# A two-block model kernel on one core: each slab product as three products of 256 columns into one sum, and two pairs of PSUM banks in turn

## The chip, the cores and the metric

One core of a Trainium2 chip. The metric is the device time of one execution in microseconds (us). The kernel before took 2976.21 us, the median of three runs (2973.67 to 2978.57).

## The reference

256 tokens of width 2048 go through four blocks of layers, all weights in fp32:

```
h = h + hybrid_layer(rmsnorm(h), ...)      # h @ w_in, gated delta rule + dilated attention, @ w_out
h = h + shortconv_layer(rmsnorm(h), ...)   # h @ w_in, short convolution, @ w_out
...                                        # second part: an input product, state-space branch,
                                           # block attention with 8 heads, gates, merge, @ w_out
h = h + ff(norm(h))                        # w_ff1 (2048 x 8192), relu(x)*x, w_ff2 (8192 x 2048)
out = rmsnorm(h)
```

Nearly all the arithmetic is weights times 256 tokens. To keep fp32 accuracy with the fast number format of the multiplying engine (fp32r), each operand is split into a high part and a low part, and a product is high*high + high*low + low*high.

## The kernel before

**Slabs and groups.** The weights stream from memory as slabs of 128x1024 fp32 (512 KB): 2 chunks of the inner dimension (k) by 4 chunks of 128 output columns (n). A ring of 4 slots holds raw slabs. ScalarE copies a slab to its high part (`wh`, L1007), VectorE subtracts to get the low part (`wl`, L1568; GpSimd does some, L1496). `walk` (L370) is the schedule of a group on ScalarE and VectorE: at each slab it splits the slab three ahead, calls hooks for the other work of the layer (two hook slots for a slab), and runs the tail of the group at places given by `tail_at`. The order of all work is written out by hand; there is no planner.

**The product.** `group` (L545) runs on TensorE. For each slab and each n it makes four products, here called a block: two with `wh` as weights (k = 0, 1) over 512 columns, which hold the high and the low part of the activations side by side, and two with `wl` over the 256 high columns. There are 3744 such blocks in the program (936 slabs by 4).

```
mm(G[n][:, :],      wh[...], rhs(k))             # 512 columns: high | low
mm(G[n][:, T:2*T],  wl[...], rhs(k)[:, 0:T])     # 256 columns, added to the second half
```

Each output chunk n has one PSUM bank `G[n]` of 512 columns: the first half is high*high, the second half the two mixed products. A group of 4, 8 or 12 slabs sums in these four banks; there are 122 groups. When it ends, `evac` on ScalarE (L1017) copies the second half of each bank to `tmp`, and `add` on VectorE (L1573) adds the first half and writes the result. Where the result goes into the residual stream, `into_x` does both steps on VectorE (L1592 or L1594, then L1600 or L1602). The add of bank n increments `bank_freed`; the next group's first product into bank n waits for it.

**Who else waits.** In the hybrid layer a head's delta rule runs beside the products of the next head, three groups (gi = 0, 1, 2) for a head, with hooks at numbered slots (`DELTA_AT`). Step 7 of the delta rule stands at slot 14, just before the second half of gi = 0's tail on VectorE: a chain of small operations (L1756, L1758, L1796). Its result goes out to memory and comes back (`act.dma_start` at L1128 to L1133, semaphore `base_moved`), and TensorE's step 10 at slot 22 (L682) waits for it. Loops are real loops on the engines (`Fori`): on TensorE one of 7 passes with three groups (heads), one of 6 passes with four groups (short convolution, L823), and several in the feed-forward part.

Of the kernel before, what the change touches and what calls it, by code (L numbers as in the profile page):

```python
# [106 lines left out]
def program(nc, stack, ins, out_d):  # L107
# [22 lines left out]
    tmp = place("tmp", [P, 4, T])  # L130
# [212 lines left out]
    tmp_ready = sem("tmp_ready")  # L343
# [43 lines left out]
    HEADS_ACT, HEADS_DVE = (1, 2), (0, 2)  # L387
    EVAC_ACT, EVAC_DVE = (1, 1), (0, 1)
# [71 lines left out]
    def group_of(pair, e):  # L460

        return 8 * (pair // 4) + 2 * (pair % 2) + pair % 4 // 2 + 4 * e

# [73 lines left out]
    def _(pe):  # L537
        mm = nc.tensor.matmul

        def group(g, q0, nslabs, rhs, ready, hook=None, slot0=0):  # L540

            for sl in range(nslabs):
# [251 lines left out]
        for gi in range(3):  # L794
            group(gi, 2 * gi, 8, xs_of, xs_wait(0), lambda slot: gates(GATE_PE.get(slot)), 16 * gi)
        pe.wait_ge(loads["hyb"], 32)

        with pe.Fori(1, QK_HEADS) as h:
            for gi in range(3):
                group(3 * h + gi, 6 * h + 2 * gi, 8, xs_of, lambda sl: None, heads(h - 1), 16 * gi)  # L800
# [8 lines left out]
        for gi in range(3):  # L809
            group(G_OUTA + gi, Q_OUTA + 2 * gi, 8, hid_of(outa_chunks), outa_ready, heads(7), 16 * gi)  # L810
        group(G_OUTA + 3, Q_OUTA + 6, 8, hid_of(outa_chunks), outa_ready)
# [5 lines left out]
        for i in range(4):  # L817
            group(G_OUTB + i, Q_OUTB + i, 4, hid_of(outb_chunks), outb_ready,
# [4 lines left out]
        with pe.Fori(0, N_SC_ITER) as j:  # L823
            for gi in range(4):
                group(G_SC + 4 * j + gi, Q_SC + 8 * j + 2 * gi, 8, xs_of, xs_wait(1))
# [5 lines left out]
        for i in range(4):  # L831
            group(G_SCOUT + i, Q_SCOUT + 3 * i, 12, lambda k: hid[:, k, :], sc_ready,
# [30 lines left out]
        for i in range(2):  # L863
            group(G_U + i, Q_U + 2 * i, 8, xs_of, xs_wait(2), before_ssm, 16 * i)
# [1679 lines left out]
```

## Time and profile before

| | before |
|---|---|
| median of 3 runs | 2976.21 us |
| the profiled execution, its own time | 2972.52 us |
| its span in the profile | 2970.7 us |
| TensorE busy | 2877.3 us (97%), 16934 products and as many weight loads |
| VectorE, ScalarE, GpSimd busy | 2170.2 us (73%), 1480.7 us (50%), 453.7 us (15%) |
| chain that ended last | TensorE 63%, "issue" 26%, VectorE 7%, ScalarE 3%, DMA 1% |
| DMA | 636.93 MB, mean 214 GB/s |

PE is TensorE's products, PEld its weight loads, which run beside the products; DVE is VectorE, ACT is ScalarE, POOL is GpSimd, SP the engine that issues most transfers. The end of a product is modelled and includes its way through the array, so neighbouring products overlap in the records: what a product costs in a stream is the distance from its start to the next one's start, not its duration. Where rows are merged (x2), the duration runs from the first start to the last end.

### The profile page before, as it was taken

The numbers are of one execution on the slowest core, as the hardware profiler recorded it, in microseconds if no ns is written. First come the engines' busy times: TensorE is split into PE (matmuls) and PEld (weight loads), VectorE is DVE, ScalarE is ACT, GpSimd is POOL, SyncE is SP. The second block draws the span as 40 slices with busy tenths as digits, with TensorE's granted clock in tenths as the row PEclk, the third lists the DMA queues.
The fourth block names the chain that finished last, engine by engine and source line by source line (L and its number), as shares of the span: only waits on it lengthen the run. The fifth ranks groups of instructions, "written<-read, shape, count | busy, mean of one in ns | idle before, by whom it ended". The sixth has DMA issues, their size and how long they took to land.

```text
span 2970.7 us, 50332 instructions
## 1 busy us (share of the span) xinstructions
PE 2877.3 (97%) x16934; PEld 2502.1 (84%) x16934; DVE 2170.2 (73%) x3182; ACT 1480.7 (50%) x2124; POOL 453.7 (15%) x188
## 2 busy tenths in 40 slices
PE   7999999999999999999999999999999999999998
PEld 6888888888888888888887877788888888888887
DVE  6677767777679888888877989976787436465466
ACT  4444444444344444444444777766544444444443
POOL 0111011111000000000000000000003445545443
PEclk9999999999999999999999999999999999999999
DMA  6544444445457888788875445556684666766655
GB/s 219 168 140 151 157 147 154 159 148 178 156 198 287 305 311 305 284 317 305 307 275 181 165 164 174 166 198 217 243 319 157 198 211 226 249 232 238 207 184 177
DMA packets 199089, 636.93 MB, mean 214 GB/s; under 512 B 32312, under 2 KB 46776, under 8 KB 198208
## 3 DMA queue, kind: packets, MB, share of 16 engines
q1 hardware_dynamic: 165024, 601.92, 58.4%
q10 hardware_dynamic: 33952, 33.52, 3.5%
q8 instruction: 69, 1.13, 0.2%
q14 instruction: 44, 0.36, 0.0%
HBM read 619.61 MB, written 15.75 MB: 214 GB/s over the span
## 4 chain that ended last, share of the span: by engine, by line
PE 63%; issue 26%; DVE 7%; ACT 3%; DMA 1%; DVEq 0%; ACTq 0%; SPq 0%; POOL 0%; POOLq 0%
PE gemm L552 39%; PE gemm L557 20%; DVE wl L1568 2%; ACT wh L1007 1%; DVE dT L1758 1%; DVE dW L1756 1%; DMA raw<-in_stream 0%; DVE qkv L1742 0%; PE side L708 0%; DVE cb L1573 0%; DVE xs L1657 0%; PE side L578 0%; DMA x<-in_x 0%; PE side L698 0%; PE side L682 0%
## 5 line engine op out<-in xcount | busy, mean ns | idle before, releaser
L552 PE MATMUL gemm<-xs,wh 128*128 128x512 f32 x5120 | 1627.6, 399 | 45.6 <-DVE cb L1573 21.2
L1007 ACT ACTIVATE wh<-raw 128x1024 fp32r<-128x1024 f32 x939 | 983.4, 1058 | 997.7 <-PE gemm L557 863.1
L1568 DVE TENSOR_TENSOR wl<-raw,wh 128x1024 fp32r<-128x1024 f32 x811 | 1034.4, 1280 | 460.1 <-ACT wh L1007 439.1
L557 PEld LDWEIGHTS gemm<-xs,wl 128*128 128x128 f32 x5120 | 965.4, 189 | 214.6
L557 PE MATMUL gemm<-xs,wl 128*128 128x256 f32 x5120 | 1015.0, 280 | 0.0
L552 PEld LDWEIGHTS gemm<-xs,wh 128*128 128x128 f32 x5120 | 781.5, 189 | 77.4 <-issue 44.0
L552 PE MATMUL gemm<-hid,wh 128*128 128x512 f32 x2368 | 745.8, 396 | 11.1 <-DVE xacc L1600 4.6
L557 PEld LDWEIGHTS gemm<-hid,wl 128*128 128x128 f32 x2368 | 446.1, 188 | 100.8
L557 PE MATMUL gemm<-hid,wl 128*128 128x256 f32 x2368 | 467.9, 279 | 0.0
L1496 POOL TENSOR_TENSOR wl<-raw,wh 128x1024 fp32r<-128x1024 f32 x128 | 349.4, 2735 | 365.3 <-ACT wh L1007 365.3
L552 PEld LDWEIGHTS gemm<-hid,wh 128*128 128x128 f32 x2368 | 357.0, 188 | 14.6 <-DVE xacc L1600 4.1
L1502 POOL TENSOR_TENSOR rn<-nrm,mhalf 128x2 f32<-128x2 f32 (+1 forms) x5 | 3.8, 760 | 1458.4 <-DVE nrm L1634 773.1
L1017 ACT ACTIVATE tmp<-gemm 128x256 f32<-128x256 f32 x408 | 152.2, 379 | 67.5 <-PE gemm L557 58.9
L1915 DVE SCALAR_TENSOR_TENSOR ada_a<-ada_a,cond 128x1024 f32<-128x1024 f32 x144 | 175.5, 1219 | 0.0
L1573 DVE TENSOR_TENSOR fx<-gemm,tmp 128x256 f32<-128x256 f32 x96 | 38.4, 421 | 80.2 <-ACT tmp L1017 78.2
L1522 POOL TENSOR_TENSOR rn<-nrm,mhalf 128x4 f32<-128x4 f32 x8 | 14.8, 1851 | 498.2 <-DVE nrm L1825 498.2
L1915 DVE SCALAR_TENSOR_TENSOR ada_b<-ada_b,cond 128x1024 f32<-128x1024 f32 x48 | 76.2, 1587 | 0.0
L2179 DVE TENSOR_TENSOR t<-side,CS 128x1024 f32<-128x1024 f32 x32 | 39.0, 1219 | 2.2 <-PE side L895 1.7
L2187 DVE TENSOR_TENSOR_SCAN rr<-mag,t 128x256 f32<-128x256 f32 x64 | 40.5, 675 | 0.0
L2192 DVE TENSOR_TENSOR crs<-rr,CS 128x1024 f32<-128x1024 f32 x32 | 39.2, 1225 | 1.1
L1742 DVE SCALAR_TENSOR_TENSOR qkv<-cb,vec,qkv 128x256 f32<-128x256 f32 x96 | 40.0, 479 | 0.0
L895 PE MATMUL side<-uT,lbt 32*128 32x256 f32 x256 | 37.2, 409 | 0.6 <-DVE lbt L2120 0.6
(393 smaller groups left out, 1801.9 us busy)
## 6 DMA issues: line engine op xcount, KB each, us to landing
raw<-in_stream SPq DMA_DIRECT2D x940, 512.0 KB, 4.1
ada_a<-in_ada SPq DMA_DIRECT2D x144, 512.0 KB, 5.2
ada_b<-in_ada SPq DMA_DIRECT2D x48, 512.0 KB, 5.3
stash<-stage ACTq DMA_DIRECT2D x12, 512.0 KB, 3.4
att<-stash ACTq DMA_DIRECT2D x8, 384.0 KB, 3.9
x<-in_x SPq DMA_DIRECT2D x4, 512.0 KB, 5.8
A_scratch<-gB ACTq DMA_DIRECT2D x8, 256.0 KB, 3.5
Dm<-D_scratch ACTq DMA_DIRECT2D x8, 256.0 KB, 3.8
```

What stands on the lines that cost most here:

```text
L552: mm(G[n][:, :], wh[:, slot, at:at + P], rhs(sl * SLAB_K + k), start=sl == 0 and k == 0, stop=False, skip_group_check=True)
L557: op = mm(G[n][:, T:2 * T], wl[:, slot, at:at + P], rhs(sl * SLAB_K + k)[:, 0:T], start=False, stop=last, skip_group_check=True)
L1007: A(wh[:, slot, :], raw[:, slot, :], ACT.Copy).then_inc(hi_ready, 1)
L1017: A(tmp[:, n, :], G[n][:, T:2 * T], ACT.Copy).then_inc(tmp_ready, 1)
L1496: nc.gpsimd.tensor_tensor(wl[:, slot, :], raw[:, slot, :], wh[:, slot, :].bitcast(F32), ALU.subtract).then_inc(lo_ready[slot], 1)
L1568: tt(wl[:, slot, :], raw[:, slot, :], wh[:, slot, :].bitcast(F32), ALU.subtract).then_inc(lo_ready[slot], 1)
L1573: tt(out, G[n][:, 0:T], tmp[:, n, :], ALU.add).then_inc(bank_freed, 1)
L1742: op = stt(qkv[:, n, :], src, w, qkv[:, n, :], ALU.mult, ALU.add)
L1915: stt(s_, s_, 0.5, cond[:, half * SLAB:half * SLAB + SLAB], ALU.mult, ALU.mult, accum_out=parts[:, bass.ds(t0 + m, 1)]).then_inc(S("ada_us ...
L2179: tt(t1[:, :, :, :], bu, CS[:, b, :, :, :], ALU.mult).then_inc(S("m_t1"), 1)
L2187: op = nc.vector.tensor_tensor_scan(rr[:, e, :], mag[:, g:g + 1].to_broadcast([P, T]), t1[:, e, 0, :], 0.0, ALU.mult, ALU.add)
L2192: tt(crs[:, b, :, :, :], rr[:, :, :].unsqueeze(2).to_broadcast([P, 2, 2, T]), CS[:, b, :, :, :], ALU.mult).then_inc(S("m_crs"), 1)
```

## The change

- A block now is six products of 256 columns, all added in the same 256 columns of PSUM: for each k `wh` times high and `wh` times low, then for each k `wl` times high. Two chunks n share a bank (columns 0 to 255 and 256 to 511).
- The four banks form two pairs. A group uses one pair; the next group uses the other. A group waits until the pair was freed by the group two before it; only the first group of a head (gi = 0) follows one on the same pair and waits for that one (`back=1`).
- `evac` on ScalarE and the buffer `tmp` are gone. On VectorE one copy of 128x512 (`take`) empties a bank, that is two chunks, and `into_x` needs one operation for each chunk.
- `bank_ready` is raised once for a group (after n = 1) in place of three times. Loops of the feed-forward part run over pairs of groups.

```diff
-        def group(g, q0, nslabs, rhs, ready, hook=None, slot0=0):
+        def group(g, pair, q0, nslabs, rhs, ready, hook=None, slot0=0, back=2):
...
                 for n in range(SLAB_N):
-                    if sl == 0:
-                        wait(pe, bank_freed, 4 * g + n - 3)
+                    if sl == 0 and n % 2 == 0:
+                        wait(pe, bank_freed, 4 * (g - back) + n + 2)
+                    o = bank(pair, n)
                     for k in range(SLAB_K):
-                        at = (k * SLAB_N + n) * P
-                        mm(G[n][:, :], wh[:, slot, at:at + P], rhs(sl * SLAB_K + k), start=sl == 0 and k == 0,
-                           stop=False, skip_group_check=True)
+                        w = wh[:, slot, (k * SLAB_N + n) * P:(k * SLAB_N + n + 1) * P]
+                        moving = rhs(sl * SLAB_K + k)
+                        mm(o, w, moving[:, 0:T], start=sl == 0 and k == 0 and n % 2 == 0, stop=False, skip_group_check=True)
+                        mm(o, w, moving[:, T:2 * T], start=False, stop=False, skip_group_check=True)
                     for k in range(SLAB_K):
-                        at = (k * SLAB_N + n) * P
+                        w = wl[:, slot, (k * SLAB_N + n) * P:(k * SLAB_N + n + 1) * P]
                         last = sl == nslabs - 1 and k == SLAB_K - 1
-                        op = mm(G[n][:, T:2 * T], wl[:, slot, at:at + P], rhs(sl * SLAB_K + k)[:, 0:T], start=False,
-                                stop=last, skip_group_check=True)
+                        op = mm(o, w, rhs(sl * SLAB_K + k)[:, 0:T], start=False, stop=last, skip_group_check=True)
                     if n == SLAB_N - 1:
                         op.then_inc(slab_used, 1)
-                    elif sl == nslabs - 1:
+                    elif sl == nslabs - 1 and n == SLAB_N // 2 - 1:
                         op.then_inc(bank_ready, 1)
...
+    def bank(pair, n):
+
+        return G[2 * pair + n // 2][:, n % 2 * T:n % 2 * T + T]
+
+    def pair_of(position):
+
+        return (position + 1) % 2
...
-        def evac(g, q_end, half=None):
-
-            for n in range(SLAB_N) if half is None else (2 * half, 2 * half + 1):
-                if n < SLAB_N - 1:
-                    act.wait_ge(bank_ready, 3 * g + n + 1)
-                else:
-                    act.wait_ge(slab_used, 4 * q_end)
-                wait(act, bank_freed, 4 * g + n - 3)
-                A(tmp[:, n, :], G[n][:, T:2 * T], ACT.Copy).then_inc(tmp_ready, 1)
...
-        def add(g, n, out):
-
-            dve.wait_ge(tmp_ready, 4 * g + n + 1)
-            tt(out, G[n][:, 0:T], tmp[:, n, :], ALU.add).then_inc(bank_freed, 1)
+        def done(g, q_end, half):
+
+            if half == 0:
+                dve.wait_ge(bank_ready, g + 1)
+            else:
+                dve.wait_ge(slab_used, 4 * q_end)
+
+        def take(g, pair, q_end, half, out):
+
+            done(g, q_end, half)
+            nc.vector.tensor_copy(out, G[2 * pair + half][:, :].rearrange("p (n t) -> p n t", n=2)
+                                  ).then_inc(bank_freed, 2)
```

**TensorE, heads loop, first slab of group gi = 1** (the program's order, with the waits; `gemm` are the banks). Before:

```order
L104 ISA
L104 REGISTER_ALU [waits hi_ready]
L104 ISA [waits lo_ready0]
L552 MATMUL gemm<-xs,wh 128x512 [waits bank_freed]
L552 MATMUL gemm<-xs,wh 128x512
L557 MATMUL gemm<-xs,wl 128x256 x2
L104 REGISTER_ALU
L552 MATMUL gemm<-xs,wh 128x512 [waits bank_freed]
L552 MATMUL gemm<-xs,wh 128x512
L557 MATMUL gemm<-xs,wl 128x256 x2
```

Now:

```order
L104 ISA
L104 REGISTER_ALU [waits hi_ready]
L559 MATMUL gemm<-xs,wh 128x256 [waits bank_freed,lo_ready0]
L560 MATMUL gemm<-xs,wh 128x256
L559 MATMUL gemm<-xs,wh 128x256
L560 MATMUL gemm<-xs,wh 128x256
L564 MATMUL gemm<-xs,wl 128x256 x2
L559 MATMUL gemm<-xs,wh 128x256
L560 MATMUL gemm<-xs,wh 128x256
L559 MATMUL gemm<-xs,wh 128x256
L560 MATMUL gemm<-xs,wh 128x256
L564 MATMUL gemm<-xs,wl 128x256 x2
```

A block went from four products to six, and the wait for a bank from every n to every second n.

**VectorE, heads loop, the end of group gi = 0** (tail, split of a slab, end of the delta rule's step 7, second half of the tail, next split). Before, two pieces: the end of the tail's first half, then the end of step 7 and the second half:

```order
L1573 TENSOR_TENSOR cb<-gemm,tmp 128x256 [waits tmp_ready]
L1565 REGISTER_ALU
L1567 REGISTER_ALU [waits hi_ready]
L1568 TENSOR_TENSOR wl<-raw,wh 128x1024 [waits slab_used]
L1756 TENSOR_TENSOR dW<-dA,dT 32x50
```

```order
L1758 TENSOR_TENSOR dT<-dT,dW 32x14 [waits dve_step]
L1796 COPY dA<-dT 32x256 [waits dve_step]
L1572 REGISTER_ALU
L1573 TENSOR_TENSOR cb<-gemm,tmp 128x256 [waits tmp_ready]
L1572 REGISTER_ALU
L1573 TENSOR_TENSOR cb<-gemm,tmp 128x256 [waits tmp_ready]
```

Now:

```order
L1748 TENSOR_TENSOR dT<-dT,dW 32x14 [waits dve_step]
L1786 COPY dA<-dT 32x256 [waits dve_step]
L1575 COPY cb<-gemm 128x2x256 [waits slab_used]
L1560 REGISTER_ALU
L1563 TENSOR_TENSOR wl<-raw,wh 128x1024 [waits slab_used,hi_ready]
```

The place of the bank's last reader is the same, behind step 7; two additions became one copy, and it no longer waits for ScalarE.

## Rows read from the trace of the kernel before

**Rows 1.** The page: busy us of each engine, share of the span, instructions.

```profile
PE 2877.3 (97%) x16934; PEld 2502.1 (84%) x16934; DVE 2170.2 (73%) x3182; ACT 1480.7 (50%) x2124; POOL 453.7 (15%) x188
```

**Rows 2.** The page, groups of instructions: line, shapes, count, busy us, mean ns, idle before.

```profile
L552 PE MATMUL gemm<-xs,wh 128*128 128x512 f32 x5120 | 1627.6, 399 | 45.6 <-DVE cb L1573 21.2
...
L557 PEld LDWEIGHTS gemm<-xs,wl 128*128 128x128 f32 x5120 | 965.4, 189 | 214.6
L557 PE MATMUL gemm<-xs,wl 128*128 128x256 f32 x5120 | 1015.0, 280 | 0.0
...
L1017 ACT ACTIVATE tmp<-gemm 128x256 f32<-128x256 f32 x408 | 152.2, 379 | 67.5 <-PE gemm L557 58.9
```

**Rows 3.** Feed-forward part: us, busy PE, PEld, DVE, ACT, POOL (x), clock, DMA share, GB/s.

```profile
2440.00:2940.00 500.00, 500.00 (x2892) 439.79 (x2891) 288.20 (x304) 230.96 (x276) 252.13 (x90) 1.00 0.64 220
```

**Rows 4.** Waits of TensorE, by whom it waited for: us in total, times, longest.

```profile
PE gemm L552 <- DVE cb L1573: 21.2, 15, 2.6
PE gemm L552 <- DVE stage L1573: 8.1, 4, 2.3
...
PE gemm L552 <- DVE xacc L1600: 4.6, 3, 3.2
...
PE gemm L552 <- DVE fxg L1573: 2.2, 1, 2.2
...
PE gemm L552 <- DVE cc L1573: 0.7, 1, 0.7
```

**Rows 5.** The timeline, 567 to 584 us (a head): start us, us, what, idle before.

```profile
570.82 0.73 PE L552 MATMUL gemm<-xs,wh 128*128 128x512 f32 x2 [0.49 <-DVE cb L1573]
...
574.60 0.73 DVE L1573 TENSOR_TENSOR cb<-gemm,tmp 128x256 f32<-128x256 f32 x2
...
575.05 0.74 PE L552 MATMUL gemm<-xs,wh 128*128 128x512 f32 x2 [2.58 <-DVE cb L1573]
575.26 1.20 DVE L1568 TENSOR_TENSOR wl<-raw,wh 128x1024 fp32r<-128x1024 f32 x1
...
577.39 0.53 ACTq L1133 DMA_DIRECT2D Em<-E_scratch  x1
...
583.36 0.98 PEld L682 LDWEIGHTS side<-Em,gB 128*128 128x128 f32 x8
```

**Rows 6.** Busy time of the engines in the state-space part.

```profile
1660.00:2000.00 340.00, 331.62 (x2056) 271.76 (x2056) 298.35 (x388) 251.37 (x411) 0.00 (x0) 0.99 0.52 175
```

**Rows 7.** The timeline of TensorE in an undisturbed stretch.

```profile
1002.58 0.40 PE L557 MATMUL gemm<-xs,wl 128*128 128x256 f32 x2
1002.82 0.62 PE L552 MATMUL gemm<-xs,wh 128*128 128x512 f32 x2
1003.28 0.39 PE L557 MATMUL gemm<-xs,wl 128*128 128x256 f32 x2
1003.50 0.62 PE L552 MATMUL gemm<-xs,wh 128*128 128x512 f32 x2
```

**Rows 8.** Three stretches behind such waits: columns as before, clock third from the end.

```profile
130.20:133.60 3.40, 3.40 (x10) 2.92 (x11) 1.37 (x2) 0.42 (x1) 0.00 (x0) 0.50 0.44 74
396.90:400.30 3.40, 3.40 (x11) 2.93 (x12) 1.39 (x2) 0.46 (x1) 0.00 (x0) 0.57 0.36 78
1710.10:1716.90 6.80, 6.80 (x23) 5.06 (x24) 5.01 (x7) 2.38 (x4) 0.00 (x0) 0.53 0.64 198
```

**Rows 9.** The DMA view of 570 to 600 us: the issue, KB, median us to landing.

```profile
Em<-E_scratch ACTq DMA_DIRECT2D x1, 256.0 KB, 4.2
```

**Rows 10.** One line's instructions: a VectorE copy that reads 512 columns of PSUM.

```profile
L2140 DVE COPY btab<-side x4: 681/684/692, 1616.8 to 1620.9; 128x512 f32<-128x512 f32 x4
```

**Rows 11.** The DMA view of 220 to 730 us: the queues beside q1.

```profile
q10 hardware_dynamic: 18094, 7.10, 5.1%
q14 instruction: 1, 0.01, 0.0%
```

**Rows 12.** The page, DMA queues: packets, MB, share of 16 engines.

```profile
q8 instruction: 69, 1.13, 0.2%
```

More of the change, by code:

```diff
@@ L1319, in _ @@
         for i in range(2):
-            walk(Q_U + 2 * i, 8, split, u_hook, 16 * i, tail=lambda half: evac(G_U + i, Q_U + 2 * i + 2, half),
-                 tail_at=EVAC_ACT)
+            walk(Q_U + 2 * i, 8, split, u_hook, 16 * i)
         def keep(gi):
@@ L1344, in _ @@
         for gi in range(12):
-            walk(Q_MIX + 2 * gi, 8, split, ssm, 16 * gi, tail=lambda half: evac(G_MIX + gi, Q_MIX + 2 * gi + 2, half),
-                 tail_at=EVAC_ACT)
+            walk(Q_MIX + 2 * gi, 8, split, ssm, 16 * gi)
         restart()
@@ L1427, in _ @@
         for n, (q, count) in enumerate(ATT_GROUPS):
-            walk(Q_ATT + q, count, split, moba, ATT_SLOT[n],
-                 tail=lambda half: evac(G_ATT + n, Q_ATT + q + count // RING, half), tail_at=HEADS_ACT)
+            walk(Q_ATT + q, count, split, moba, ATT_SLOT[n])
             if n >= 4:
@@ L1450, in _ @@
         for i in range(4):
-            walk(Q_MRG + i, 4, split, merge(i), tail=lambda half: evac(G_MRG + i, Q_MRG + i + 1, half),
-                 tail_at=EVAC_ACT)
+            walk(Q_MRG + i, 4, split, merge(i))
             act.wait_ge(S("mrg"), i + 1)
@@ L1990, in out @@
                 def out(half):
[L1991 to L1992 removed]
+                    take(G_SC + g, pair_of(gi), Q_SC + 2 * g + 2, half, (cc, uu, uu, cc)[gi][:, 2 * half:2 * half + 2, :])
                 walk(Q_SC + 2 * g, 8, split, convs(j, gi, beside(20 * j, ADA_SC, 8 * gi)), pool=POOL_NONE,
@@ L2147, in out @@
             def out(half):
-                for n in (2 * half, 2 * half + 1):
-                    add(G_U + i, n, uT[:, 4 * i + n, :])
+                at = 4 * i + 2 * half
+                take(G_U + i, pair_of(i), Q_U + 2 * i + 2, half, uT[:, at:at + 2, :])
             walk(Q_U + 2 * i, 8, split, before_ssm, 16 * i, POOL_NONE, tail=out, tail_at=EVAC_DVE)
@@ L2205, in out @@
                     wait(dve, loads["stash"], 16 * gi)
-                for n in (2 * half, 2 * half + 1):
-                    add(G_MIX + gi, n, stage[:, n, :])
+                take(G_MIX + gi, pair_of(gi), Q_MIX + 2 * gi + 2, half, stage[:, 2 * half:2 * half + 2, :])
             walk(Q_MIX + 2 * gi, 8, split, ssm, 16 * gi, POOL_NONE, tail=out, tail_at=EVAC_DVE)
@@ L2266, in out @@
                     dve.wait_ge(loads["stash2"], 16)
-                for c in (2 * half, 2 * half + 1):
-                    add(G_ATT + n, c, late_out(n)[:, c, :])
+                take(G_ATT + n, pair_of(n), Q_ATT + q + count // RING, half, late_out(n)[:, 2 * half:2 * half + 2, :])
             walk(Q_ATT + q, count, split, moba, ATT_SLOT[n], POOL_NONE, tail=out, tail_at=HEADS_DVE)
@@ L2275, in out @@
             def out(half):
-                for c in (2 * half, 2 * half + 1):
-                    add(G_MRG + i, c, mt[:, c, :])
+                take(G_MRG + i, pair_of(i), Q_MRG + i + 1, half, mt[:, 2 * half:2 * half + 2, :])
             walk(Q_MRG + i, 4, split, pool=POOL_NONE, tail=out, tail_at=EVAC_DVE)
@@ L2312, in _, with ff_in, out @@
         scale3 = scaling(3, norm_g)
-        def ff_in(c, i, hook=None):
+        def ff_in(c, i, half, hook=None):
             g = G_FF + 8 * c + i
-            def out(half):
-                for n in (2 * half, 2 * half + 1):
-                    add(g, n, fx[:, n, :])
+            def out(part):
+                take(g, pair_of(half), Q_FF + 16 * c + 2 * i + 2, part, fx[:, 2 * part:2 * part + 2, :])
             walk(Q_FF + 16 * c + 2 * i, 8, split, hook, tail=out, tail_at=EVAC_DVE)
@@ L2326, in ff_in, with ff_out, both @@
             low(o[:, :, T:2 * T], mt[:, :, :], o[:, :, 0:T]).then_inc(S("ff_lo"), 1)
-        def ff_out(c, i, out, hook=None):
+        def ff_out(c, i, half, out, hook=None):
             g = G_FF + 8 * c + 4 + i
-            def both(half):
-                for n in (2 * half, 2 * half + 1):
-                    add(g, n, out(n))
+            def both(part):
+                take(g, pair_of(half), Q_FF + 16 * c + 8 + 2 * i + 2, part, out(2 * part))
             walk(Q_FF + 16 * c + 8 + 2 * i, 8, split, hook, tail=both, tail_at=EVAC_DVE)
@@ L2365, in _ @@
         mods(80, 96)
-        with dve.Fori(0, 4) as i:
+        with dve.Fori(0, 2) as i2:
             restart()
-            ff_in(FF_QUARTERS - 1, i)
+            for half in range(2):
+                ff_in(FF_QUARTERS - 1, 2 * i2 + half, half)
         for i in range(4):
```

121 lines of the change are left out of this document (52 added, 69 removed).

## The prediction

> **What bounds the kernel now.** I read the busy shares first [rows 1]: TensorE is busy 97% of the span, so only two things can change the time: what a block of products costs, and when TensorE stands still. The costliest groups [rows 2] name the products. Their durations can't be added (399 and 280 ns overlap their neighbours), so I take the block from a stretch without side work: 500.00 us with 2892 products [rows 3] are 723 blocks of four, **0.6916 us a block**. 3744 blocks are 2589 us, 87% of the span. Then the list of TensorE's waits [rows 4] for what stands between blocks, and the timeline for where and why [rows 5]. VectorE is at 73% on the whole, but 298 of 340 us in the state-space part [rows 6]; where it is late, TensorE waits for a bank.
>
> **Part 1, the block: four products become six.** The columns stay: 2 x 512 + 2 x 256 = 1536 = 6 x 256. The question is what a product of 256 costs when it follows another one and each brings its own weight load. Rows show it for the `wl` products: 2560 pairs are busy 1015.0 us [rows 2], 0.3965 us a pair, less one duration of 0.280 gives 0.1165 us from the first start to the second. From the first start to the next block's start two of them take 0.24 and 0.22 us [rows 7], 0.115 each. I take 0.116 for each of six: 0.696 against 0.6916, +0.0044 x 3744 = **+16 us**. Lower bound: cost goes by columns alone, 0 us. Upper bound from these rows: all six at 0.1165, 0.699, +28 us. No row shows more than two such products in a row, nor five that add to the same 256 columns one behind the other; the first of the two `wl` products, which is followed by one on the same columns, is the dearer.
>
> Here a rule can be weighed. The rows give a 512-column product (0.6916 - 0.232)/2 = 0.230 us and a 256-column one 0.116, so nearly all of the cost goes by columns. The Trainium skill (TensorE: Matmul & The Clock Gate, "Back-to-back issue gap") gives N/2.4 ns plus 2.5 ns fixed for each product, which speaks against this change: two more products a block are 5 ns, +19 us by that page's figure, and the sum below would be 3 us higher. The trace's slope is steeper than the page's (0.230 against 0.216 us for 512 columns), so the page's absolute gap isn't used.
>
> **Part 2, the waits for banks that go.** TensorE's waits for a bank are 21.2 us in 15 (cb), 8.1 in 4 (stage), 4.6 in 3 (xacc) [rows 4], and five more lines of the same list, from fxg (2.2) to cc (0.7), give 7.3 us in 7: 41.2 us in 29. The idle time is counted after a modelled end; the real one is 0.280 - 0.116 = 0.16 us earlier, and after the wait the load isn't hidden. The timeline shows that in the start distances: the first product's pair lasts 0.73 or 0.74 us where it is 0.62 or 0.63 elsewhere [rows 5, 7], 0.11 more. 29 x 0.27 = 8 us. Behind three of these waits the granted clock is at the lower of its two levels, 1.2 GHz, for nearly all of 3.4, 3.4 and 6.8 us (0.50, 0.57 and 0.53 with the edges) [rows 8]; half of 13.6 us is 7 us. Gross: 41 + 8 + 7 = **-56 us**. Both causes fall away. The next group writes the other pair, which was emptied a whole group (8 slabs of 4 x 0.69 = 22 us) ago. At the head's edge, where the same pair is used again, the list has no wait for `bb`, the output written there, and the order of the tail is kept.
>
> What is late next? PE runs on into slabs that are ready (three ahead). The old group ended at 570.82 - 0.49 - 0.16 = 570.2 [rows 5]; without the waits TensorE gets to slab 3 of the new one at 570.2 + 3 x 2.77 = 578.5, and that slab's split comes right behind the tail, at 575.26 [rows 5]. So no slab wait follows. But **step 10 of the delta rule** does: its transfer is issued at 577.39 [rows 5] and takes 4.2 us [rows 9], so it lands at 581.6. TensorE came there at 583.36. Per head 0.49 + 2.58 + 2 x 0.27 = 3.6 us go, TensorE comes at 579.8 and waits 1.8 us; 8 heads give back **+15 us**. The chain in front of that transfer is VectorE's step 7, which stands before the tail's second half and does not move. Bounds: 0 (if it comes 2 us sooner) and 8 x 3.6 = 29 us. In the state-space part VectorE stays at 88%, so some of the 8.1 us there may come back: +3 us, between 0 and 8.
>
> **Part 3, work that goes from other engines.** ScalarE loses 408 copies, 152.2 us [rows 2], at 50% busy: 0 on the end. VectorE's pair of additions takes 0.73 us [rows 5]; the copy of 512 columns from PSUM is priced by such a copy at 0.684 us [rows 10], so VectorE gains 0.05 us a half, 11 us over 204 halves, beside TensorE: 0. What it hides behind is TensorE's block time; if that cover were gone, it would still be a gain. `into_x` halves its operations: gain, hidden too. No DMA is added or moved.
>
> **Sum.** -56 + 15 + 3 + 16 = -22 us. The profiled execution took 2972.52 us (span 2970.7), so 2950.5; the median is 3.7 us above that execution, so I forecast **2954 us**. The forecast's own range: gains from -56 to -20, block from 0 to +28: 2930 to 2972, the ends not all at once.
>
> **Rivals.**
> 1. *The weight load becomes the bound* (slower). Today two loads serve 768 columns, then three. Each 256-column product must hide one, and the heads' eight loads of 128 columns take 0.98 us [rows 5]: less the 0.189 of one [rows 2], 0.113 us from load to load. That leaves 3 ns to 0.116. In a steady row of six, with loads and products in lockstep, or with sums into the same columns 256 columns apart, the distance could be 0.118 us or more. At 0.118: 22464 x (0.118 - 0.1153) = +61, less 38 of gain, +23: 2999 us. It decides from 0.1170 us on (38/22464 = 0.0017 above 0.1153), only 0.0005 above a row, so this is a real case. Against it: eight loads in a row do hold 0.113.
> 2. *The waits move instead of going.* All chains that TensorE now runs into (step 10, the state-space scans, the attention steps) hold it as long as the banks did: -56 + 50 + 16: 2986 us, at most. For it: step 10 alone can return half of a head's gain. Against it: TensorE is idle 93 us in all [rows 1], 41 of them for banks, so at its norms, slabs and hooks together it waits 52 us today.
> 3. *The loops no longer stay in TensorE's instruction memory.* In the heads loop the instruction queue q8 carries nothing in 510 us [rows 11], though 69 come over the span [rows 12]: the loop's code stays. The loops grow by half; the largest from 1024 loads and products to 1536. If the head of a loop had to be fetched at each pass, about 13 passes would each wait for something like a transfer's 4.2 us [rows 9]: +50, 3004 us, of which shorter waits are as likely. The Trainium skill (Runtime: NRT & Kernel Launch, "Instruction fetch mechanics") gives TensorE room for 2048 instructions and says that a branch to code outside it stalls; by that page's figure the loop fits, and no run here shows it yet.
> 4. *More comes back than I count*: the banks' waits go, step 10 doesn't wait, the block costs by columns: 2976 - 56 + 6 = 2926 us.
> 5. That the change doesn't do what it says: each product might share its weights with the one before, so that six products need four loads. In the trace there are as many loads as products [rows 1], also where weights repeat, so I expect six; fewer would only remove rival 1.
>
> **How the numbers follow.** Forecast 0.56, rival 1 0.16, rival 2 0.13, rival 3 0.08, rival 4 0.07. About 0.2%, 6 us, is what a measurement of this kernel can tell from no change: faster means under 2970. Faster: 0.53 of the forecast's cases, 0.07 of rival 4, 0.02 of rival 2: 0.62. Same (to 2982): 0.03 + 0.04 of rival 1, 0.04 of rival 2, 0.03 of rival 3: 0.14. Slower: 0.24. Range 2931 to 2998: it leaves out the far ends of rivals 1, 3 and 4.
>
> **What would show it.** Waits of TensorE for a bank gone from the list, or a few left at a head's edge. A new wait of TensorE at L688 (step 10's line there) with about 15 us in 8. In 500 us of the feed-forward part 4310 products (0.116 us each) if I am right, 4338 if cost goes by columns; under 4274 rival 1 has won. q8 near 69 x 1.5 = 103 packets, and none within a loop; many more would be rival 3. No cold stretch behind the head's tail. I am wrong in the main if the block costs over 0.702 us or if the waits of TensorE still sum to more than 60 us.

## The result, and the profile after

| | before | after |
|---|---|---|
| median of the runs | 2975.08 us (2973.67 to 2978.57, 4 runs) | 3017.62 us (3010.75 to 3019.33, 4 runs) |
| the profiled execution | 2972.52 us, span 2970.7 | 3010.75 us, span 3008.9 |

The ratio is 1.0137 (95% interval 1.0118 to 1.0155): the change makes the kernel 1.4% slower, 42 us. The forecast was 2954 us in a range of 2931 to 2998. The time lies outside it, on the other side of the kernel before.

The busy shares come first, from the page of the kernel after; they answer to [rows 1]:

```profile
PE 2912.7 (97%) x24422; PEld 2857.8 (95%) x24422; DVE 2143.3 (71%) x2898; ACT 1348.0 (45%) x1716; POOL 435.0 (14%) x188
```

Each product still has its own weight load (24422 of both), so rival 5 is out. TensorE's idle time is 3008.9 - 2912.7 = 96 us; it was 93 [rows 1]. So of the 38 us by which the profiled executions differ, 35 lie in *busy* time, and the idle time, from which most of the gain was to come (41 of the 56 us of part 2), is where it was. What it is made of is in the list of TensorE's waits. Each row is the engine, tile and line that waited, whom it waited for, then us in total, times and the longest:

```profile
PE gemm L559 <- issue: 20.7, 11, 2.8
PE side L688 <- DMA Em<-E_scratch: 15.0, 8, 3.8
PE side L584 <- DVE sq L1670: 13.2, 1, 13.2
...
PE side L672 <- DVE qkv L1761: 6.3, 8, 0.9
PE side L714 <- DVE Wm L1799: 4.9, 7, 0.7
...
PE side L769 <- ACT vnat L1159: 3.5, 8, 0.5
...
PE side L938 <- DVE mSb L2239: 2.7, 1, 2.7
```

- The waits for a bank (41.2 us in 29, led by the rows cb, stage and xacc of [rows 4]) are gone from the list.
- The new wait at L688 is the one forecast, 15.0 us in 8 where the prediction has "about 15 us in 8". The timeline below shows it for one head: the transfer is issued at 584.49, and TensorE starts at 588.57, after 1.04 us without work.
- L672 and L769, chains inside a head, hold TensorE for 9.8 us in 16. They are in no row of before.
- "issue" is 20.7 us in 11, with gaps up to 2.8 us. In the kernel before that row has 2.8 us in 5. Nothing in the profile shows what these wait for; the next view does.

The timeline at one such gap, and then at one of those transfers (start, us, engine, line, what; idle time before it in brackets):

```profile
982.79 0.40 PE L564 MATMUL gemm<-xs,wl 128*128 128x256 f32 x2
985.77 0.38 PE L559 MATMUL gemm<-xs,wh 128*128 128x256 f32 x1 [2.58 <-issue]
...
986.94 0.41 PE L560 MATMUL gemm<-xs,wh 128*128 128x256 f32 x1
987.16 0.63 PE L564 MATMUL gemm<-xs,wl 128*128 128x256 f32 x2
...
991.33 0.28 PE L559 MATMUL gemm<-xs,wh 128*128 128x256 f32 x1 [0.98 <-issue]
```

```profile
584.49 0.53 ACTq L1136 DMA_DIRECT2D Em<-E_scratch  x1
588.57 0.97 PEld L688 LDWEIGHTS side<-Em,gB 128*128 128x128 f32 x8 [1.24 <-DMA Em<-E_scratch]
588.57 1.16 PE L688 MATMUL side<-Em,gB 128*128 128x128 f32 x8 [1.04 <-DMA Em<-E_scratch]
```

The gap before 985.77 is followed, from 986.9 on, by products of 0.41 us in place of 0.28 (the lower clock), and 5.6 us later by a second gap. The long gap comes back near 1082, 1177, 1272 and 1368, about 95 us apart, which is one pass of the short-convolution loop (the second gap too, except at 1177), and a single one of 2.8 us stands in the feed-forward part, at 2638.5, where the outer loop jumps back. The queue q8 carries instructions. The page's row of q8 (packets, MB, share), and the DMA view's row for 940 to 1400 us, which holds five of these places:

```profile
q8 instruction: 157, 2.57, 0.3%
```

```profile
q8 instruction: 43, 0.70, 0.6%
```

157 packets stand against 69 before [rows 12] and the 103 that larger code alone would give. Much of the rest comes in the short-convolution part: in the same 460 us the kernel before has 2 packets. In the heads loop, between 187 and 743 us, the kernel after still has none.

Last the pace of the products, from the view that gives each stretch a row: us, then busy us and count of PE, PEld, DVE, ACT, POOL, then clock, DMA share, GB/s. The first row answers to [rows 3]; then come five stretches in which TensorE is never idle, a cold stretch behind a loop gap, and the first and third stretch of [rows 8]:

```profile
2440.00:2940.00 500.00, 497.17 (x4248) 496.97 (x4247) 275.76 (x237) 198.79 (x190) 236.26 (x89) 1.00 0.64 219
2365.00:2450.00 85.00, 85.00 (x724) 85.00 (x723) 27.02 (x24) 33.47 (x32) 37.09 (x15) 1.00 0.57 187
2555.00:2635.00 80.00, 80.00 (x682) 80.00 (x681) 42.01 (x40) 29.72 (x28) 36.89 (x15) 1.00 0.71 247
2735.00:2815.00 80.00, 80.00 (x708) 80.00 (x708) 48.37 (x41) 32.10 (x31) 41.23 (x16) 1.00 0.70 241
2912.00:2992.00 80.00, 80.00 (x709) 80.00 (x707) 46.32 (x48) 35.09 (x34) 39.83 (x16) 1.00 0.59 191
820.00:880.00 60.00, 60.00 (x531) 60.00 (x531) 36.91 (x44) 27.73 (x26) 0.00 (x0) 1.00 0.65 212
2638.90:2642.30 3.40, 3.40 (x19) 3.40 (x18) 1.42 (x1) 0.00 (x0) 0.34 (x1) 0.51 0.56 188
130.20:133.60 3.40, 3.40 (x31) 3.40 (x30) 3.10 (x11) 0.31 (x1) 0.00 (x0) 1.00 0.53 164
1710.10:1716.90 6.80, 6.80 (x59) 6.41 (x57) 5.40 (x9) 5.87 (x10) 0.00 (x0) 1.00 0.43 134
```

4248 products in 500 us, under the 4274 from which the prediction says that rival 1 has won. But the window also holds the gap at 2638.5 (2.8 us idle) and the 3.4 us of lower clock behind it, together some 38 products; without them it would be 4286. The short rows say more (about two of each count began before the stretch). Between 2365 and 2450 a product takes 85/722 = **0.1177 us**, between 2555 and 2635 80/680, the same; in the other three 80/706, 80/707 and 60/529 = **0.1133 us**. There is hardly anything between these two values: from the starts of all products in the trace, taken block by block where nothing interrupts them (3112 of the 3744 blocks), 84% of the blocks take 0.7067 us and 16% take 0.6800. Their mean is 0.7025 us a block; taken in the same way, the kernel before has 0.6916. And 2555 to 2635 and 2735 to 2815 run the same instructions, the products of one loop with `hid` as the moving operand, in its two passes.

The last two rows show what did work: the stretches behind two of the old bank waits run at the full clock now, which is 2.4 GHz of its two levels.

### The profile page after: what moved, and what is told of

It is laid out like the page before. It is cut to its first block, busy times and chain, and to the rows that moved or that the text cites. A ratio compares the mean times of both kernels' runs of the same rounds, so it can differ in the third digit from the quotient of the medians.

```text
span 3008.9 us, 63937 instructions
## 1 busy us (share of the span) xinstructions
PE 2912.7 (97%) x24422; PEld 2857.8 (95%) x24422; DVE 2143.3 (71%) x2898; ACT 1348.0 (45%) x1716; POOL 435.0 (14%) x188
## 4 chain that ended last, share of the span: by engine, by line
PE 63%; issue 26%; DVE 6%; ACT 3%; DMA 2%; ACTq 0%; DVEq 0%; POOL 0%; SPq 0%; POOLq 0%
PE gemm L559 20%; PE gemm L560 20%; PE gemm L564 19%; DVE wl L1563 2%; ACT wh L1020 1%; DMA Em<-E_scratch 1%; DVE dT L1748 1%; DVE dW L1746 1%; DMA E_scratch<-dA 1%; DVE qkv L1732 0%; PE side L688 0%; PE side L714 0%; DVE xs L1647 0%; DMA x<-in_x 0%; PE side L704 0%
## 5 line engine op out<-in xcount | busy, mean ns | idle before, releaser
L1020 ACT ACTIVATE wh<-raw 128x1024 fp32r<-128x1024 f32 x939 | 986.9, 1059 | 1160.3 <-PE gemm L564 1036.0
L559 PE MATMUL gemm<-xs,wh 128*128 128x256 f32 x5120 | 1350.6, 286 | 31.1 <-issue 18.6
L560 PE MATMUL gemm<-xs,wh 128*128 128x256 f32 x5120 | 1325.1, 281 | 0.0
L559 PEld LDWEIGHTS gemm<-xs,wh 128*128 128x128 f32 x5120 | 967.8, 189 | 52.2 <-issue 51.4
L560 PEld LDWEIGHTS gemm<-xs,wh 128*128 128x128 f32 x5120 | 967.6, 189 | 5.9 <-issue 5.3
L564 PEld LDWEIGHTS gemm<-xs,wl 128*128 128x128 f32 x5120 | 786.9, 189 | 0.0
L559 PE MATMUL gemm<-hid,wh 128*128 128x256 f32 x2368 | 609.0, 281 | 4.3 <-DVE wl L1563 2.1
L560 PE MATMUL gemm<-hid,wh 128*128 128x256 f32 x2368 | 604.6, 279 | 0.0
L559 PEld LDWEIGHTS gemm<-hid,wh 128*128 128x128 f32 x2368 | 447.4, 189 | 5.3 <-issue 2.7
L560 PEld LDWEIGHTS gemm<-hid,wh 128*128 128x128 f32 x2368 | 446.1, 188 | 0.1
L1491 POOL TENSOR_TENSOR wl<-raw,wh 128x1024 fp32r<-128x1024 f32 x128 | 337.6, 2642 | 389.1 <-ACT wh L1020 389.1
L564 PEld LDWEIGHTS gemm<-hid,wl 128*128 128x128 f32 x2368 | 360.5, 188 | 0.0
L1575 DVE COPY fx<-gemm 128x512 f32<-128x512 f32 x48 | 33.0, 687 | 85.6 <-PE gemm L564 85.6
L1459 ACT ACTIVATE hid<-mt 128x1024 f32 (+1 forms) x16 | 17.0, 1061 | 69.0 <-DVE mt L2307 69.0
```

The lines of the kernel that those rows point to most:

```text
L559: mm(o, w, moving[:, 0:T], start=sl == 0 and k == 0 and n % 2 == 0, stop=False, skip_group_check=True)
L560: mm(o, w, moving[:, T:2 * T], start=False, stop=False, skip_group_check=True)
L564: op = mm(o, w, rhs(sl * SLAB_K + k)[:, 0:T], start=False, stop=last, skip_group_check=True)
L1020: A(wh[:, slot, :], raw[:, slot, :], ACT.Copy).then_inc(hi_ready, 1)
L1459: A(hid2[:, 4 * i:4 * i + 4, 0:T] if isinstance(i, int) else hid2[:, bass.ds(4 * i, 4), 0:T], mt[:, :, :], ACT.Copy).then_inc(S("ff_hi"), 1)
L1491: nc.gpsimd.tensor_tensor(wl[:, slot, :], raw[:, slot, :], wh[:, slot, :].bitcast(F32), ALU.subtract).then_inc(lo_ready[slot], 1)
```

## The experiments

I had three theories of the loss. **A**: a short product is dearer by itself. By the pace above, a block costs 0.011 us more than the 0.6916 of before, 3744 times: 41 us. **B**: the pace is slow because products follow one another on the *same* PSUM columns (one sum of six in place of two). **C**: the loops that got longer are fetched again at each pass, and TensorE stands still for it. A and B are two readings of the same microseconds; C is beside them.

**1. Only the products are split.** The kernel before, with its banks, its two sums and its copies, and the 512-column product as two (so its loops get longer too):

```diff
-                        mm(G[n][:, :], wh[:, slot, at:at + P], rhs(sl * SLAB_K + k), start=sl == 0 and k == 0,
+                        moving = rhs(sl * SLAB_K + k)
+                        mm(G[n][:, 0:T], wh[:, slot, at:at + P], moving[:, 0:T], start=sl == 0 and k == 0,
+                           stop=False, skip_group_check=True)
+                        mm(G[n][:, T:2 * T], wh[:, slot, at:at + P], moving[:, T:2 * T], start=False,
```

> The kernel before with one edit: the wh product of 512 columns is issued as two of 256 into the two halves of its bank; banks, waits, copies and additions stay. Theory A (a 256-column product in a steady row with its own weight load costs 0.1178 us in place of 0.1153, in whatever columns it sums): blocks of 0.7067 us, 3744 x 0.015 = +56 us, plus about 22 us of stalls at the back jump of the four-group loop, since the loop is as long as the changed kernel's: 3045 to 3055 us. Theory B (the extra cost comes from sums into the same 256 columns one behind the other, which here happens for 2 of 6 products only): blocks of at most 0.697 us, 3000 to 3020 us.

Measured: 3028.16 us (3026.74 to 3028.57), ratio 1.0182 (1.0165 to 1.0199). The split alone, with the longer loops that it brings (143 packets of q8), makes the whole loss and more. In this kernel only two of six successions stay on the same columns, and its pace is the slow one all the same, in the stretch of the first short row above:

```profile
2365.00:2450.00 85.00, 85.00 (x723) 85.00 (x723) 29.83 (x34) 38.33 (x47) 38.20 (x16) 1.00 0.60 195
```

So B falls. My size for A was too high by about 20 us.

**2. No two products in a row on the same columns.** The changed kernel, with the chunks n and n + 1 of a bank in turn:

```diff
+                        for part in range(2):
+                            for n in two:
+                                product(n, wh, k, slice(part * T, part * T + T),
+                                        first=sl == 0 and k == 0 and part == 0 and n % 2 == 0)
```

> The changed kernel with the products of chunks n and n+1 taken in turn, so that no product adds to the columns of the one before it. Theory B (same columns in a row cost the extra 4.4 ns): blocks fall from 0.7067 to 0.692 us or less, about -50 us: 2965 us. Theory A (load and product in lockstep): no change, 3010 to 3020 us.

Measured: 3026.89 us (3012.74 to 3031.51), ratio 1.0166 (1.0135 to 1.0198), not faster than the change as it is. Its blocks run at the same two levels, with a mean of 0.702 us. B is out from this side too.

**3. Short loops.** The changed kernel, with the short-convolution loop as 12 passes of two groups in place of 6 of four, and TensorE's outer feed-forward loop written out:

```diff
-        with pe.Fori(0, N_SC_ITER) as j:
-            for gi in range(4):
+        with pe.Fori(0, 2 * N_SC_ITER) as jj:
+            for gi in range(2):
...
-        with pe.Fori(1, FF_QUARTERS - 1) as c:
+        for c in range(1, FF_QUARTERS - 1):
```

> The changed kernel with shorter loops on TensorE alone: the short-convolution loop has 12 passes of two groups in place of 6 of four, and the outer loop of the feed-forward quarters is written out. Theory C (the long loop does not stay in TensorE's instruction memory): the stalls of 2.6 to 3.1 and 1.2 to 1.5 us at 986, 1082, 1177, 1272, 1368 and 2638 us go, about 22 us: 2990 to 2997 us, and q8 falls from 157 packets to about 110. If those stalls had another cause: 3010 to 3020 us.

Measured: 2993.89 us (2989.29 to 3004.67), ratio 1.0062 (1.0044 to 1.0080), 24 us less than the change (its profiled run is its longest, 3004.67 us). The same window of the short-convolution part in the three kernels, before, after and with short loops, columns as above:

```profile
940.00:1400.00 460.00, 456.91 (x2635) 400.83 (x2634) 398.48 (x542) 209.54 (x255) 0.00 (x0) 1.00 0.83 305
```

```profile
940.00:1400.00 460.00, 443.22 (x3688) 441.88 (x3687) 371.36 (x467) 173.16 (x164) 0.00 (x0) 0.98 0.80 286
```

```profile
940.00:1400.00 460.00, 459.28 (x3892) 458.42 (x3891) 391.18 (x495) 180.38 (x172) 0.00 (x0) 1.00 0.81 302
```

3892 - 3688 = 204 products more in the same time are 24 us. Of those, 459.28 - 443.22 = 16 us are idle time that went; the clock, 0.98 of full speed and then 1.00, carries most of the rest (460 x 0.02 = 9 us). q8 carries 1 packet here in place of 43, and 106 in the whole program, close to the 103 that the prediction gave for code half as large again. TensorE's row of waits for "issue" is back at the value before:

```profile
PE side L688 <- DMA Em<-E_scratch: 25.3, 8, 4.0
...
PE gemm L559 <- issue: 2.8, 6, 1.1
```

C is shown, with its size. The first row is a surprise: in this profiled run step 10 waits 25.3 us where the change had 15.0. The page's row of that transfer has a median of 6.0 us to landing in place of 4.2 [rows 9]:

```profile
Em<-E_scratch ACTq DMA_DIRECT2D x8, 256.0 KB, 6.0
```

**4. What a product costs.** The kernel before with rows of 32 more products at its end, each with its own 128x128 weights, of 512, 384, 320, 288, 256 and 192 columns. Those of 256 come in four kinds (adding to the same columns, overwriting them, in two halves of a bank in turn, in two banks in turn). Then eight times the old block's order, and 32 with the same weights (L1009). One run, 3022.72 us with the added rows.

> The kernel before with rows of 32 products of fp32r added before the last norm, each with its own 128-column weight load: 512 columns; 256 into the same columns, adding and overwriting; 256 into two halves of a bank in turn; 256 into two banks in turn; 384; 320; 288; the order 512, 512, 256, 256; 256 with the same weights each time; 192. Theory A (load bound below some width): 192 and 256 columns at the same 0.113 to 0.118 us, 288 near it, 384 and 512 by columns (0.170, 0.227). Theory B: adding into the same columns 0.1178, the other three rows of 256 columns 0.113. By columns alone: 192 at 0.086, 256 at 0.115, 320 at 0.144.

The rows with one form to a line show the way of reading: 32 starts span 3.99 us less the last one's duration.

```profile
3000.80 3.99 PE L1009 MATMUL side<-hid 128*128 128x256 f32 x32
3004.63 3.72 PE L986 MATMUL side<-hid 128*128 128x192 f32 x32
```

(3.99 - 0.28)/31 = 0.120 us for 256 columns with weights that stay the same, and (3.72 - 0.25)/31 = 0.112 us for 192 columns. The other rows are merged in that view; from the start of each product in the trace:

```
columns   ns from start to start    columns / 2.4 GHz    difference
512       227                       213.3                13 to 14
384       173.3                     160.0                13.3
320       146.7                     133.3                13.3
288       131.9                     120.0                12
256       120.0 in all four kinds   106.7                13.3
192       111.7                      80.0                32
block 512, 512, 256, 256:           about 697            57 / 4 = 14
```

From 512 down to 256 columns a product costs its columns at 2.4 GHz and about 13 ns beside. Only below 256 columns does something else bound it, at 0.112 us, and that is near the 0.113 from load to load that the prediction read from [rows 5]. So the load's own pace of 0.112 us does *not* set the 0.120 of a 256-column product; it is the fixed part, paid six times in place of four. Neither the columns that it writes, nor overwriting or adding, nor the weights change that. But every product of these rows has a load, also where the weights stay the same (32 loads at L1009), so no row tells how much of the 13 ns is the load's. The Trainium skill (TensorE: Matmul & The Clock Gate, "Back-to-back issue gap") has a fixed part of 2.5 ns, but for a product by itself; for a stream of loads and products, as here, it gives some 131 ns at 512 columns. For these fp32r products the trace agrees with neither: 13.3 ns and 227 ns.

**5. The split, with short loops.** Experiment 1 with the short-convolution loop of two groups. It is the price of the split without C.

> The kernel before with the 512-column product split in two as in the run split_only, and the short-convolution loop as 12 passes of two groups: banks, waits, copies as before, and no loop longer than 1200 instructions or so. The price of the split product alone: per block 0.7033 against 0.6916 us in the split_only profile, 3744 x 0.0117 = +44 us: 3018 us. Against the run small_loops (2994 us) it tells what the pairs of banks, the single sum and the single copy give when nothing else differs: about 24 us if the waits for banks go (56 us) and about 30 come back at step 10 and other hooks; near 0 if all of it comes back.

Measured: 3011.79 us (2999.42 to 3012.51), ratio 1.0109 (1.0089 to 1.0130). So the two more products cost 3011.8 - 2975 = 37 us (some 7 of them by the clock: in the profiled executions it stands at the lower level for 41 us before the last norm, where the kernel before has 27), and what the bank pairs, the single sum and the one copy bring *together* is 3011.8 - 2993.9 = 18 us (experiment 3 has them, experiment 5 hasn't; experiment 3 also has the feed-forward loop written out). The prediction had counted 56 of gains less 18 that come back.

**6. Step 10 later.** Experiment 3, with steps 10 to 17 of the delta rule one or two hook slots later, so that step 10 stands at slot 24 and not at 22:

```diff
-        (0, 2, 4, 5, 8, 10, 12, 14, 17, 19, 22, 23, 24, 25, 26, 27, 28, 30, 32, 34, 37, 39, 41))}
+        (0, 2, 4, 5, 8, 10, 12, 14, 17, 19, 24, 25, 26, 27, 28, 29, 30, 31, 32, 34, 37, 39, 41))}
```

> The run small_loops with steps 10 to 17 of the delta rule two hook slots later on all engines (24 to 31), so 2.8 us more between the issue of the transfer and TensorE's wait for it. If the waits at step 10 (25.3 us in 8 in that profile) are time given back, they fall to under 5 us and the kernel gains 10 to 20 us: 2975 to 2984 us. If they only cover waits that come next (the chain of steps 11 to 17 on VectorE), the same waits appear at the later steps: 2990 us or more.

Measured: **2956.14 us** (2946.36 to 2962.91), ratio 0.9925 (0.9904 to 0.9947). It is the best of all kernels here, 0.75% under the kernel before and 61 us under the change. The waits for `Em` from memory are gone; one of 2.3 us in 8 for VectorE is in their place. The timeline shows a transfer issued at 571.78 and used at 577.42, with no idle time before. Under it stand the first 1000 us of two kernels in columns as above, first experiment 3, then this one:

```profile
571.78 0.53 ACTq L1136 DMA_DIRECT2D Em<-E_scratch  x1
577.42 0.97 PEld L688 LDWEIGHTS side<-Em,gB 128*128 128x128 f32 x8
```

```profile
0.00:1000.00 1000.00, 938.45 (x7714) 924.61 (x7715) 705.13 (x1183) 408.60 (x584) 94.99 (x57) 0.98 0.52 171
```

```profile
0.00:1000.00 1000.00, 964.37 (x8083) 951.18 (x8084) 740.23 (x1224) 427.05 (x602) 95.00 (x57) 1.00 0.55 185
```

8083 - 7714 = 369 products more in the same time are 43 us. 26 of them are idle time that went (964.37 - 938.45), and the other 17 go with the clock, which was 0.98 and is 1.00: in experiment 3 it stands at the lower level for 34 us of these 1000, here never. So these waits cost 1.7 times their own length. I had expected 2975 to 2984; the part that I left out is the clock behind the waits.

**7. The old kernel, with its head's tail one step sooner.** If the waits for `cb` are all that the banks were good for, a cheaper change takes them away: the kernel before with the second half of the head's tail one slab sooner.

```diff
-    HEADS_ACT, HEADS_DVE = (1, 2), (0, 2)
+    HEADS_ACT, HEADS_DVE = (1, 1), (0, 1)
```

> The kernel before with the second half of the heads' tail on ScalarE and VectorE moved ahead of the hook at slot 14 (step 7 of the delta rule), nothing else. TensorE's waits for the bank behind cb (2.6 us in each of 8 heads, 2.9 with the load and the pipeline) go, and the waits at step 10 come: it comes 2.9 us sooner, 580.5 against a landing at 581.6 us, so 1.1 us of it is given back. 8 x 1.8 plus two cold stretches of 1.7: -10 to -18 us, 2960 us. If the transfer then collides with slab loads as in the changed kernel (6.0 us in place of 4.2), all but 0 to 4 us come back.

Measured: 2990.07 us (2989.06 to 2995.15), ratio 1.0053 (1.0039 to 1.0067): slower, where I had expected 2960 or, with a slower transfer, about the time of before. The two rows of its list of waits show why; they answer to the first of [rows 4]:

```profile
PE side L682 <- DMA Em<-E_scratch: 24.2, 8, 3.5
...
PE gemm L552 <- DVE cb L1573: 2.9, 7, 0.5
```

18.3 us of bank waits went, and 24.2 us for step 10 came. The transfer takes 6.0 us to land in the heads loop where the kernel before has 4.3, and behind the waits the clock drops, here after the head at 138:

```profile
138.40:141.80 3.40, 3.35 (x13) 3.15 (x14) 1.23 (x3) 0.00 (x0) 0.00 (x0) 0.50 0.62 194
```

**8. Both together in the old kernel.** Experiment 7 with the later steps of experiment 6.

> The run before_tail with steps 10 to 17 two hook slots later, as in late_step. If step 10's wait is what gives time back there, this version is the faster one by up to 9 us more: 2950 to 2957 us, below both kernels. If the later steps only move the wait to VectorE's chain: as before_tail.

Measured: 2967.16 us (2959.72 to 2969.23, 9 runs), ratio 0.9969 (0.9960 to 0.9979): faster than before by 0.3%, with two tables of numbers changed, and less than I expected (2950 to 2957). A part of the wait only moved on: in this kernel TensorE waits at L718 for VectorE's `Em`, 12.7 us in 8.

**9 and 10. The later steps alone.** They were put into the kernel before and into the change, with nothing else.

> The kernel before with steps 10 to 17 of the delta rule one or two slots later, nothing else. It tells what part of the gain of the two late kernels is the later steps themselves. My account: in the kernel before TensorE comes to step 10 at 583.4, after the transfer has landed, so there is no wait to take away: 2975, within 6 us either way, and waits for the banks cb of about 21 us as before. Rival: the later steps also gain elsewhere (cold clock behind the waits, other steps of the head): 2960 or less; then the gain of the late kernels over the kernel before is not that of the change.

> The changed kernel with the same later steps, its long loops kept. By the account (3018, less 15 us of waits for Em and half of 3.4 us of cold clock behind some of them) 2990 to 3003, with the stalls behind the loops' back jumps and about 157 q8 packets still there. If the later steps were worth to it what they were worth beside the short loops (38 us between medians) it is 2980. If nothing beyond the 15 us were behind them, 3003.

Measured: the kernel before with later steps 2975.09 us (2972.14 to 2978.04, 11 runs), ratio 0.9999 (0.9990 to 1.0008): no difference. It has the same row for `cb`, 21.2 us in 15. The change with later steps: 2987.60 us (2979.46 to 2999.14, 6 runs), ratio 1.0034 (1.0021 to 1.0047), 30 us less than the change itself and somewhat below the 2990 to 3003 that I had expected, with q8 still at 157 packets and

```profile
PE gemm L559 <- issue: 19.6, 9, 3.7
```

The two profiled executions, the shortest run of the change and the longest of this kernel, differ by 11.6 us only; what makes up the rest of the 30 is in no profile.

So the later steps aren't a gain of their own. They are worth nothing where the banks hold TensorE back, and 23 (experiments 7 and 8) to 38 us where they don't. The gain of experiment 6 needs the change, once its two side effects are mended; but experiment 8 comes within 11 us of it with the old products. Short loops were not tried in the kernel before by themselves; its TensorE waits for "issue" are 2.8 us in all, so there is little for them to take away.

All the medians in one table, in us:

```
                         loops as they are     short loops
before                   2975                  -
before, later steps      2975                  -
before, split            3028                  3012
after                    3018                  2994
after, later steps       2988                  2956
```

## Why the prediction was wrong

Both things by which the prediction would be "wrong in the main" came: the block costs over 0.702 us, if by little, and TensorE's waits sum to more than 60 us (96 us idle). By the medians it is 64 us off. The block (41 us in place of 16), the loops (24 in place of 0, experiment 3) and step 10 with what hangs on it (30 in place of 15, experiment 10) make up these 64; they come from different runs, so that the sum fits to the microsecond is luck.

**The block (part 1): wrong, and the main step.** "I take 0.116 for each of six" gave +16 us. It is 0.1171: 3744 x (0.7025 - 0.6916) = +41 us, above even the upper bound of +28, and close to the 37 of experiment 5. The value and the upper bound came from the two `wl` products of the old block, which follow products of 512 columns: 0.115 and 0.1165 us. Six short ones in a row run at 0.1133 or 0.1177, and mostly at the slower. The prediction named the trap (no row shows more than two such products in a row) and still drew the upper end from those two. A better bound was in [rows 2, 3]: the old block of 0.6916 us has 1536 columns, which at 2.4 GHz are 0.640, so four products carry 0.0516 of fixed cost, 0.0129 each. Six at that price are 0.640 + 6 x 0.0129 = 0.717 us, +97 us for the program. The real figure lies between the two readings, and the range should have held both. Inside the kernel the fixed part came to (0.7025 - 0.640)/6 = 0.0104 us a product, less than in the old block and in the rows of experiment 4; why wasn't settled.

**Rival 1** got its number (decides from 0.1170 us) but not its mechanism. It has the weight load as the bound, or sums into the same columns. The load's floor is 0.112 us, below both levels (the faster, 0.1133, is near it), and B fell twice. That a load adds to each product's fixed part isn't excluded.

**The banks (part 2): right.** All 29 waits are gone, and the two cold windows of [rows 8] that are shown above run at the full clock. That the sum is 56 us was not measured by itself; the account below holds with 49 and the clock apart.

**Step 10: right in place and cause, and in size** in the profiled execution (15.0 us in 8, bounds 0 to 29). The size is partly luck: behind the five transfers that took 4.0 to 4.3 us the waits are 1.0 to 1.6 us, not 1.8, and behind the three of 5.4 to 6.8 us they are 2.5 to 3.8. Two things were missing: that the new wait brings cold stretches of its own, as the one at 498.8 to 502.2 us (clock 0.50 in that window), and that the transfer takes up to 6.8 us when it comes at another time. In experiment 10 these waits, with what hangs on them, are worth 30 us. I had costed the clock behind the waits that go and not behind the one that comes.

**The waits move (rival 2): in part.** With L672, L769 and L938, some 10 us in all, inner chains of a head and of the attention part hold TensorE now; I had +3 for the state-space part, where nothing came back. (In rival 4 the +6 has no source.)

**Loops (rival 3, chance 0.08): it came true, at half its price.** The prediction had 13 passes at 4.2 us (55 us, where it writes 50). There are six places, each with a gap of 2.3 to 2.8 us and a cold stretch, four of them with a second gap of about 1 us: 24 us. "The loops grow by half" also misses one: the outer feed-forward loop went from 512 loads and products to 1536, since its inner loops now hold pairs of groups, and the gap at 2638.5 is its back jump. The Trainium skill (Runtime: NRT & Kernel Launch, "Instruction fetch mechanics") gives room for 2048 instructions, by which the loops would fit. The trace doesn't agree: the short-convolution loop has 1536 loads and products and about 1620 instructions with its waits, and it doesn't stay; the heads loop, with about 1540, does. The same section says that a taken branch stalls where its target is outside the current window of two pages, 256 instructions each. That doesn't agree either: the old loop of 1024 loads and products is longer, and q8 carries 2 packets in 460 us of it. Sizes between 1540 and 1620 were not tried.

**Copies (part 3): right.** `take` is 0.687 us against the 0.684 forecast [rows 10], beside TensorE:

```profile
L1575 DVE COPY fx<-gemm 128x512 f32<-128x512 f32 x48 | 33.0, 687 | 85.6 <-PE gemm L564 85.6
```

The account against the profiled execution of before, whose span is 38.2 us shorter: bank waits with the hidden part of each -49, block +41, step 10 with its hidden part +17, loop fetches +20 (18 in the row, and 0.16 us more at each, as the modelled end hides it), inner chains +10, clock +3 ((1 - 0.993) x 3008.9 against (1 - 0.994) x 2970.7; the bank waits' cold stretches went and others came). The sum is +42, 4 more than measured. For experiment 6, with a span of 2961.1: -49, block 0.7028 us +42, inner chains +8, clock 0.996 for -6: -5, where -9.6 was measured.

**What stays open** is what sets the level of 0.1133 or 0.1177 us. It holds for many microseconds, differs between two passes over the same code, and differs between kernels with the same products: the 706 that take 80.0 us from 2735 on in the kernel after take 83.15 us in experiment 6. Of the 62 changes of level in the kernel after, all but one have a gap, a side product or a longer block between the two levels. All of it at the faster level would be worth 0.84 x 3744 x 0.0267 = 84 us. It may be why the runs of most split kernels scatter more (8.6 us here and 16.6 in experiment 6, but 1.8 in experiment 1, where the kernel before has 5); that was not shown.

## What to carry to other kernels

Cost a product by its columns *and* by its number: what short products cost is read from a long row of them, and until one is measured, the range takes in the fixed cost that the present block shows, times the new count. When a wait goes, the loops that grew and the latency that it hid must be looked at together with it: this change was worth -19 us, not +42 (and -11 against the old kernel with two tables changed), once the loops were short enough to stay in TensorE's instruction memory and one step that depends on a transfer stood two slots later. And a table of such slots is tuned to the waits around it: moved alone, it gained nothing in the kernel before and 30 us in the one after.

## What the runs showed of the hardware

- A product of 128x128 weights (fp32r), with a weight load each time, costs its columns at 2.4 GHz and 12 to 14 ns, from 512 down to 256 columns (227 to 120 ns); at 192 columns it takes 0.112 us. In the kernel's rows of six a 256-column product runs at 0.1133 or 0.1177 us, each for long stretches.
- A loop on TensorE of about 1620 instructions is fetched again at each pass: a gap of 2.3 to 2.8 us, mostly a second of 1.0 us some 5.6 us later, and a clock of 0.50 between them. One of about 1540 isn't.
- The 256 KB transfer `Em` takes 4.3 us in the kernel before, 4.0 to 6.8 in the kernel after and 6.0 in two others (experiments 3 and 7), issued at another time against the slabs' transfers. That the slabs are the cause was not tried by itself.
- A wait of 2.2 to 4 us on TensorE is often followed by 3.4 or 6.8 us at half clock: 7 of the 8 at step 10 in experiment 3, 3 of 12 in the kernel before (from 100 us on). Half of that time comes on top of the wait.
